# Half of the tokens of an expert layer computed densely over streamed tables, instead of gathering 128 expert rows for each token

## The reference

```
q = (hf @ w_q).reshape(T, 8, 2, 128)
s = jnp.einsum('thpd,hpnd->thpn', q, sub_keys)
sc, idx = lax.top_k(s, 16)
cand = sc[:, :, 0, :, None] + sc[:, :, 1, None, :]           # 256 sums a head
cidx = idx[:, :, 0, :, None] * 128 + idx[:, :, 1, None, :]
top_sc, pos = lax.top_k(cand, 16)
eidx = jnp.take_along_axis(cidx, pos, axis=-1)
gate = jax.nn.softmax(top_sc, axis=-1)
act = jax.nn.gelu(jnp.einsum('thkd,td->thk', u_tab[eidx], hf))
y = jnp.einsum('thk,thkd->td', gate * act, v_tab[eidx])
out = rms_norm(h + g2 * y, final_g)
```

## Time and profile before

| | |
|---|---|
| time, median of 3 runs | 3458.14 us (3454.32 to 3459.94) |
| span of the profiled execution | 3452.1 us |
| busy: PE, DVE, ACT, POOL | 91%, 60%, 31%, 56% of the span |
| last stage (first to last indirect DMA) | 2132.4 to 3416.6 us |
| DMA in the last stage | 411 GB/s |

### The profile page before, as it was taken

The page is one execution under the profiler, slowest core; times in us unless marked ns, Lnnn a source line. Parts: engine busy times, 40 slices in busy tenths (PEclk is TensorE's granted clock), DMA queues, the critical chain, the costliest instruction groups (busy, mean ns, idle before and its releaser), DMA issues.

```text
span 3452.1 us, 34902 instructions
## 1 busy us (share of the span) xinstructions
PE 3142.6 (91%) x12254; PEld 2099.6 (61%) x12254; DVE 2087.5 (60%) x3701; ACT 1062.6 (31%) x2577; POOL 1917.9 (56%) x1198
## 2 busy tenths in 40 slices
PE   7999999999999999999999999999978787777776
PEld 5778778887766888868777677544433333333332
DVE  5764453336764433479556776777667676666654
ACT  4564441112165211120132432333333332333222
POOL 4545259997403899968767565444444444434432
PEclk9999999999999999999999999999999999999999
DMA  4430022232311222323413124999999999999997
GB/s 164 171 134 1 13 86 98 97 120 74 134 62 49 90 95 96 115 71 124 140 62 115 50 80 172 421 421 419 422 415 412 421 421 421 421 421 420 421 421 299
DMA packets 108994, 741.68 MB, mean 215 GB/s; under 512 B 11816, under 2 KB 12968, under 8 KB 20776
## 3 DMA queue, kind: packets, MB, share of 16 engines
q0 software_dynamic: 73728, 536.90, 37.5%
q1 hardware_dynamic: 31488, 196.25, 16.2%
q10 hardware_dynamic: 3624, 6.56, 0.5%
HBM read 731.28 MB, written 8.39 MB: 214 GB/s over the span
## 4 chain that ended last, share of the span: by engine, by line
PE 63%; DMA 21%; DVE 8%; ACT 4%; issue 2%; POOL 2%; DVEq 0%; POOLq 0%; ACTq 0%
DMA arena<-in_peer_uv,rstd 15%; PE bank L1298 13%; PE bank L1299 13%; PE bank L1300 13%; PE bank L1814 8%; DMA weight_ring<-in_peer_uv,rstd 3%; DMA normed<-in_peer_uv,rstd 2%; DVE arena L3295 2%; PE bank L1829 1%; PE bank L1744 1%; PE bank L1726 1%; PE bank L1612 1%; PE bank L1490 1%; PE bank L1245 1%; PE bank L1500 1%
## 5 line engine op out<-in xcount | busy, mean ns | idle before, releaser
L1155 POOL DMA_INDIRECT arena<-in_peer_uv,rstd x419 | 456.4, 1089 | 622.0 <-PE bank L1814 570.3
L3295 DVE CUSTOM_DVE_ANT_0 arena<-arena,branch 128x1024 f32<-128x1024 f32 x419 | 510.5, 1225 | 333.5 <-DMA arena<-in_peer_uv,rstd 327.5
L1300 PE MATMUL bank<-split_arena 128*128 128x512 f32 x1776 | 695.1, 391 | 0.0
L1066 POOL TENSOR_TENSOR split_arena<-weight_ring,ones 128x1024 fp32r<-128x1024 f32 x204 | 506.6, 2483 | 151.0 <-PE bank L1300 99.3
L1298 PE MATMUL bank<-split_arena 128*128 128x512 f32 x1392 | 546.6, 393 | 5.6 <-DVE split_normed L2697 2.5
L1299 PE MATMUL bank<-split_arena 128*128 128x512 f32 x1392 | 542.3, 390 | 0.0
L1068 POOL TENSOR_TENSOR split_arena<-weight_ring,split_arena 128x1024 fp32r<-128x1024 f32 x204 | 519.3, 2545 | 16.0
L1814 PE MATMUL bank<-arena,row_diagonals 128*128 128x512 f32 x836 | 397.8, 618 | 92.0 <-ACT row_diagonals L2425 91.7
L1814 PE MATMUL bank<-arena,level_mask 128*128 128x512 f32 x840 | 392.0, 608 | 75.0 <-ACT level_mask L2425 74.7
L1300 PEld LDWEIGHTS bank<-split_arena 128*128 128x128 f32 x1776 | 334.0, 188 | 73.6
L1035 POOL TENSOR_TENSOR split_arena<-weight_ring,split_arena 128x1024 fp32r<-128x1024 f32 x54 | 129.5, 2406 | 401.2 <-ACT split_arena L1980 349.3
(11 more groups left out here) (490 smaller groups left out, 4921.4 us busy)
## 6 DMA issues: line engine op xcount, KB each, us to landing
weight_ring<-in_w_up SPq DMA_DIRECT2D x32, 1024.0 KB, 4.9
weight_ring<-in_w_down SPq DMA_DIRECT2D x32, 1024.0 KB, 4.9
weight_ring<-in_w_in SPq DMA_DIRECT2D x32, 1024.0 KB, 5.0
weight_ring<-in_ada_w SPq DMA_DIRECT2D x24, 1024.0 KB, 4.9
weight_ring<-in_w_in_a SPq DMA_DIRECT2D x12, 1024.0 KB, 6.4
weight_ring<-in_w_out SPq DMA_DIRECT2D x12, 1024.0 KB, 6.9
weight_ring<-in_w_in_b SPq DMA_DIRECT2D x10, 1024.0 KB, 5.9
arena<-in_peer_uv,rstd POOLq DMA_INDIRECT x419
```

The costliest lines, as they stand in the source:

```text
L1066: pool.tensor_tensor(hi, part, bc_mid(ones[:], DT), ALU.mult).then_inc(split_hi, 1)
L1155: pool.indirect_dma_start(row_slots[slot_of[r]], None, a["peer_uv"], bass.IndirectOffsetOnAxis(ap=experts[n % 2][:, c:c + 1], axis=0)).the ...
L1300: return pe.matmul(psum[t.bank][:], hi, a_lo[k], start=False, stop=last)
L3295: dve.tensor_tensor_reduce(row, row, h_tok[:, r // NE, :], 1.0, 0.0, ALU.mult, ALU.add, dots[:, i % 4, j:j + 1]).then_inc(dot_ready, 1)
```

## The change

Blocks 0 and 1 (256 tokens) still gather their 256 rows. Blocks 2 and 3 (256 tokens, `DENSE`) are computed against all 16384 experts: u and v are laid out a second time, as 128 units each of 128x1024 (512 KB; unit j holds the experts whose second key is j), and stream through four buffers (`raws`). ScalarE copies a unit to its high part (`raw_top`), GpSimd subtracts for the low part (`raw_rest`, since `low_by` returns 0 for every unit), and TensorE multiplies: `up_unit` has 24 fp32r matmuls of 256 columns, `down_unit` 12 of 512. Between the two stand Gelu (`activate`) and the product with a dense matrix of gates, zero where a token has not chosen an expert. That matrix is made by 64 "gate" steps: one-hot matrices of the first key by GpSimd (`first_ones`, 8 instructions) and of the second by VectorE (`second_ones`), scaled by ScalarE, multiplied on TensorE, and folded in by VectorE (`gate_weights`).

The program of the last stage is now: 32 groups of two rows as before (64 rows, all of block 0, with all query work for all blocks packed beside them), and then 320 steps in the list `STEPS`: 64 u units (steps 0 to 63); 32 gate steps (64 to 95); 64 v units and 64 u units in turn (96 to 223); 32 gate steps (224 to 255); 64 v units (256 to 319). The other 192 rows ride along in them, by `row_step`: 24 in steps 4 to 63, 12 in the first gate steps, 96 in steps 96 to 223, 12 in the second gate steps, and 48 in the 56 steps from 256. These late rows have 2, then 3, then 4 slots, and their second half is now VectorE's (`late_add`) instead of TensorE's. Of the searches, 59 pieces stand beside the 32 groups, and 66 pieces at one a step from step 0.

```diff
-NROW = TT * NE
-NGRP = NROW // GROUP
+SUMMED = 64
+NGRP = SUMMED // GROUP
+LATE = 2 * NE - SUMMED
+DENSE = 2 * P
+RAWS = 4
+PAIRS = 3
...
+        piece_count = [1 if 2 <= i <= 12 else 0 if i in (0, 13, 14) else 2 if i <= 21 else 3 if i <= 27 else 4 for i in range(NGRP)]
...
+                    low_wait(sp, n - RAWS)
+                sp.dma_start(raws[n % RAWS], a["peer_vd" if value else "peer_ut"][m]).then_inc(raw_landed[n % RAWS], 16)
...
+            def raw_rest(n):
...
+                hi, lo = pairs_of[n % PAIRS]
+                pool.wait_ge(raw_high, n + 1)
+                pool.tensor_tensor(lo, raws[n % RAWS], f32(hi), ALU.subtract).then_inc(raw_low[0], 1)
...
+            def late_gather(x):
...
+                if before is not None:
+                    pool.wait_ge(late_acc, before + 1)
...
+                pool.indirect_dma_start(late_slots[i], None, a["peer_uv"],
...
+                for x in range(GTOK):
+                    m = pool.tensor_scalar(one_first[v % 2][:, x, :], iota_key, index_t[b][:, 0, GTOK * t + x:GTOK * t + x + 1], None,
+                                           ALU.is_equal)
...
+            for s, (kind, v) in enumerate(STEPS):
+                if kind == "item":
+                    raw_rest(v + 2)
+                else:
+                    first_ones(v)
+                for x in gathers_at[s]:
+                    late_gather(x)
...
+                for k in range(DT):
...
+                    pe.matmul(psum[t.bank][:, 0:DENSE], hi[:, k, :], dense_hi[:, k, :], start=k == 0, stop=False)
+                    pe.matmul(psum[t.bank][:, 0:DENSE], hi[:, k, :], dense_lo[:, k, :], start=False, stop=False)
+                    m = pe.matmul(psum[t.bank][:, 0:DENSE], lo[:, k, :], dense_hi[:, k, :], start=False, stop=k == DT - 1)
...
+                for b in range(2):
+                    for w, part in ((w_hi, hi), (w_hi, lo), (w_lo, hi)):
+                        for c in range(2):
+                            x = pe.matmul(psum[2 * b + c][:], blk(w, b), part[:, 512 * c:512 * (c + 1)],
...
+                act.wait_ge(raw_landed[n % RAWS], 16 * (n // RAWS + 1))
+                if n >= PAIRS:
+                    act.wait_ge(item_done, n - PAIRS + 1)
...
+                act.activation(pairs_of[n % PAIRS][0], raws[n % RAWS], ACT.Copy).then_inc(raw_high, 1)
...
+                dve.tensor_tensor(w_lo, weights[:, :, m % WHALF], f32(w_hi), ALU.subtract).then_inc(w_low, 1)
...
+                dve.wait_ge(late_landed[gather_slot[x]], 16 * gather_fill[x])
+                dve.tensor_tensor_reduce(row, row, h_tok[:, n, :], 1.0, 0.0, ALU.mult, ALU.add,
+                                         late_dots[:, x % 8:x % 8 + 1]).then_inc(late_dot, 1)
...
+                dve.wait_ge(late_gate, x + 1)
...
+                    m = dve.scalar_tensor_tensor(acc[n], row, w, acc[n], ALU.mult, ALU.add)
```

More of the change, by code:

```diff
@@ L105, in build @@
         ring = sb("weight_ring", [P, RING, UNIT_K * UNIT_N])
+        with nc.sbuf_tensor("split_residual", [P, DT, SEQ], F32R) as split_X:
+            pass
         X = sb("residual", [P, DT, SEQ])
@@ L562, in build @@
                 n, x = turn_at[i]
[L563 to L573 removed]
+                tok_turns[n].append(aux(2 + x))
@@ new lines, in build, with item_of @@
+            for n, g in score_at.get(i, ()):
+                plan_scores(n, g, 4 + g % 2)
+        LAST_SCORES = [(2, 3, 6), (3, 3, 7), (1, 0, 2), (1, 1, 3)]
+        for n, g, bank in LAST_SCORES:
+            plan_scores(n, g, bank)
+        def item_of(m, value):
+            if not value:
+                return m if m < WHALF else m + (m - WHALF) + 1
+            return WHALF + 2 * m if m < WHALF else NKEY + m
+        ITEMS = [None] * (2 * NKEY)
+        for m in range(NKEY):
+            ITEMS[item_of(m, False)] = (False, m)
+            ITEMS[item_of(m, True)] = (True, m)
@@ new lines, in build @@
+        G_FIRST = {0: item_of(0, True), 1: item_of(WHALF, True)}
+        STEPS = []
+        for n in range(2 * NKEY):
+            for half, at in G_FIRST.items():
+                if n == at:
+                    STEPS += [("gate", half * NGATE + q) for q in range(NGATE)]
+            STEPS.append(("item", n))
+        step_of = {x: s for s, x in enumerate(STEPS)}
+        V_LAST = step_of["item", G_FIRST[1]]
+        late_score_at = {10: (1, 2, 6), 18: (1, 3, 7)}
+        index_at = {21: 0, 35: 1}
@@ L576, in build @@
+        v_tiles = [item_tile(2 * NKEY - 1, b) for b in range(4)]
         q_f = region(0, LH)
@@ new lines, in build @@
+        G_AT = [step_of["gate", half * NGATE] for half in range(2)]
+        row_step = []
+        for first, last, count_ in ((4, G_AT[0], 24), (G_AT[0], G_AT[0] + NGATE, 12), (G_AT[0] + NGATE, G_AT[1], 96),
+                                    (G_AT[1], V_LAST, 12), (V_LAST, V_LAST + 56, 48)):
+            row_step += [first + i * (last - first) // count_ for i in range(count_)]
+        first_gather = {0: -1, 1: -1, 2: 22, 3: G_AT[0]}
+        gather_step = [first_gather[gather_slot[x]] if gather_prev[x] is None else row_step[gather_prev[x]] + 2 for x in range(LATE)]
@@ new lines, in gate_products @@
+            def gate_products(v):
+                t = gate_tiles[v]
+                pe.wait_ge(first_hot, v + 1)
+                pe.wait_ge(gate_hot, v + 1)
+                free(pe, t)
+                for x in range(GTOK):
+                    m = pe.matmul(psum[t.bank][:, x * WHALF:(x + 1) * WHALF], one_first[v % 2][:, x, :], one_second[v % 2][:, x, :],
+                                  start=True, stop=True)
+                m.then_inc(psum_full, 1)
+            for s, (kind, v) in enumerate(STEPS):
+                if kind == "gate":
+                    gate_products(v)
+                elif ITEMS[v][0]:
+                    down_unit(v, ITEMS[v][1])
+                else:
+                    up_unit(v, ITEMS[v][1])
+                if s in late_score_at:
+                    key_scores(*late_score_at[s][0:2])
+                if s in index_at:
+                    b = index_at[s]
+                    pe.wait_ge(turn_in, sum(k[0] >= 2 and searched[k] <= searched[2 + b, 3] for k in SEARCHES))
+                    turn(index_tiles[b], [firsts[2 + b], seconds[2 + b], gates[2 + b]])
+                if s == GAIN_AT:
@@ L3312, in _ @@
-            add_rows(TT - 1)
-            finish_rows(TT - 1)
+                pieces(i)
+            for k in range(DT):
+                dve.wait_ge(dense_high, k + 1)
+                dve.tensor_tensor(dense_lo[:, k, :], H[:, k, DENSE:], f32(dense_hi[:, k, :]), ALU.subtract).then_inc(dense_split, 1)
+            for x, t in enumerate(row_sums):
+                full(dve, t)
+                dve.tensor_copy(acc[0][:, 512 * x:512 * (x + 1)], psum[t.bank][:]).then_inc(bank_out[t.bank], 1)
+            for t in row_sums:
+                have(dve, t)
```

632 lines of the change are left out of this document (455 added, 177 removed).

## The result

The changed kernel takes 3966.51 us (median of 4 runs, 3964.59 to 3970.1) against 3458.71 us for the kernel before, measured beside it: a ratio of 1.1472 [1.1456, 1.1488], 14.7% slower. The forecast was 3790 us, with a range to 3900. The direction was right; the time is 176 us over the forecast and 67 us over the range.

A forecast was written before the change was run, and what follows sets the result against it. DMA bound the last stage before; then VectorE and GpSimd taking turns would. 2141.6 + 240 + 12 + 275 + 211 + 584 + 302 + 18 = 3784 us, with 6 us around it 3790 us; range 3660 to 3900.

The forecast's parts named there:

- the 3.25 us: Average time for each of the 320 steps at which the whole time would stay as it was.
- The 32 groups and the bubble: Start of the last stage: 240 us for 32 two-row groups, then 12 us until the first units reach TensorE.
- Turns of VectorE and GpSimd: In the 320 steps, two-input VectorE instructions and GpSimd subtractions exclude each other; a 512-element instruction costs the pair 0.54 us.
- Steps 96 to 223: 128 units, 96 rows and 64 weight splits: 4.56 us a step, 584 us (545 to 666).
- the gate steps: 64 steps making the dense gates: chain of 3.3 us a step, one-hot instructions 2.4 for eight; 211 us (166 to 256).
- The rival on the clock: TensorE falls to 1.2 GHz from idling: units of 5.2 to 5.6 us, 4030 us in all; chance 0.03.
- Steps 256 to 319: Last 64 units, 48 rows in the first 56: 5.0 us a step, then 8 x 2.8; 302 us (284 to 341).
- late adds... low parts behind those, then TensorE: In the steps, later VectorE adds would delay gathers in GpSimd's queue, then low parts, then TensorE; no size given.
- Steps 0 to 63: First 64 units with 24 rows and 64 pieces of searches: 4.3 us a step, 275 us (240 to 326).
- The expectation on halves: With every second low part on VectorE: 3.9, 3.8 and 4.6 us a step, 3810 us in all.
- theory C: In steps 96 to 223, which VectorE instruction waits behind a subtraction counts: 3.8 to 3.9 us a step, 3840 us in all.
- The rival of tighter turns: Over all 320 steps, each subtraction precedes a waiting VectorE instruction and gathers wait under products: 3870 to 4010 us; chance 0.17.

The follow-up runs named there:

- e3: Changed kernel with all low parts but the first two subtracted by VectorE, not GpSimd: 3816.13 us, 1.1034 of the kernel before.
- e2: Changed kernel with products and adds of the 192 late rows replaced by one-input sums (part of the result left out): 3803.93 us, one run.
- e1: Changed kernel with first-key one-hot matrices made by one VectorE instruction a gate step, not eight of GpSimd: 3870.39 us, 1.1195 of the kernel before.
- e10: e1 with half of the gate matmuls (gates of half of the dense tokens left out): 3814.47 us, 1.1033 of the kernel before.
- e5: Changed kernel with a late row's ScalarE work one step later and its add behind the next product: 3950.61 us, 1.1428 of the kernel before.
- e4: Changed kernel with every second low part, after the first two, subtracted by VectorE: 3925.85 us, 1.1354 of the kernel before.
- e7: Changed kernel with low parts of v units alone subtracted by VectorE, u units by GpSimd: 3890.05 us, 1.1253 of the kernel before.
- e8: Changed kernel with the edits of e1, e5 and e7 together: 3705.73 us, 1.0718 of the kernel before.

## Why the prediction was wrong

- **Direction and bound.** Right. DMA ceased to be the bound, and a step costs more than the 3.25 us that would have kept the time.
- **The 32 groups and the bubble.** TensorE began the first unit at 2378.0 us instead of 2393.6, 16 us better than forecast. It was idle for 6.0 us before it, where 12 were put. What it waited for in this bubble is a VectorE instruction of 32 elements, held as long as GpSimd subtracted (VectorE, then GpSimd):

```profile
2370.29 7.26 DVE L3574 TENSOR_TENSOR rstd<-squares 128x32 f32<-128x32 f32 x1
...
2370.54 4.66 POOL L1289 TENSOR_TENSOR split_residual<-weight_ring,split_residual 128x1024 fp32r<-128x1024 f32 x2
2375.14 2.34 POOL L1289 TENSOR_TENSOR split_arena<-weight_ring,split_arena 128x1024 fp32r<-128x1024 f32 x1
```

  Its median over the run is 0.19 us. It began 0.25 us before the first of three subtractions, got no turn between them, and ended 0.07 us after the third. In e3, with two subtractions there, it took 4.97.
- **Turns of VectorE and GpSimd.** Right, and shown: e2 takes the second input away, and e3 the subtractions, and either gives back 150 to 163 us. Steps 96 to 223 took 4.39 against 4.56 us. TensorE was 74% busy there at a clock of 0.94, not near 60% at full clock, but it was not the bound. For the semaphores (0.4 in the gate steps, and in the 0.9 behind a product) the forecast had no row; the trace has VectorE idle for 0.60 us behind a product. The forecast spread the waits over the product, the add and a small part of the splits; in the trace the splits and adds have them, and VectorE also waits before the splits.
- **The step that failed: the gate steps.** "The one-hot instructions of GpSimd have no row; 128 elements at the rate of L1035 are 0.30 us, 2.4 for eight, and 0 to 2.4 bound it." They take 0.593, 4.74 for eight. The rate per element of a 1024-element instruction was carried down to 128 elements, and from a subtraction of two tensors to a TENSOR_SCALAR. The instruction takes 0.29 us more than that. Whether this is a fixed cost of each instruction or a slower rate of this one, no run tells, as all have the same size. And the estimate was made the upper bound as well, so that the range had no room for it, though the forecast itself counted the gate steps among its weakest terms. GpSimd's sum, 4.74 + 0.4 for gathers, went over the chain of 3.3, and the bound moved to another engine. e1, which takes it away, gives back 84 us; e2, which takes the turns away, 41.
- **The clock in the gate steps**, the second part of the same term. "TensorE 16 x 0.117 = 1.9" took full clock; the granted clock is 0.50 in both stretches and the 16 records of a step take 3.6. The rival on the clock was weighed for the unit steps, where it came in small part (0.87 to 0.94), and not for the gate steps. It was no bound while GpSimd took 4.74. Without that a step takes 4.6, and e10 shows that TensorE has a share in it; with 3.6 us of TensorE for each step at this clock, 3.3 was out of reach in any case.
- **Steps 256 to 319.** 37 us too low. The sum added up turns, while a loop through four queues takes 5.64 us for each step with a row; e5 breaks it for 32 us. The forecast had the way in which a wait spreads ("late adds... low parts behind those, then TensorE") but gave it no price.
- **Steps 0 to 63.** 17 us too low; VectorE busy 276 of 292 us. Against e3, the durations of its instructions other than subtractions add up to 90 us more: 30 in the products and adds of rows, and 60 in instructions of the searches, of which TENSOR_SCALAR and CAST read one tensor. The forecast had put 0.5 us a step for a piece's two-input instructions.
- **The expectation on halves** (e4, and theory C of e7) failed too: that of e4 took waits as proportional to the number of subtractions. The account of VectorE's queue above fits e3, e4 and e7 within 3 us, but it is read from their own traces. In e8 it gives 150 us for 63 subtractions, 2.4 each.
- **The rival of tighter turns.** The measured time lies in its range (3870 to 4010), but not by its mechanism: it had 326, 256, 666 and 341 us for the four parts, and 292, 379, 561 and 339 were measured.

A gather beside VectorE was weighed in the prediction. In e7 one begins under a product that ends at 3104.61, another under a plain TENSOR_TENSOR that ends at 3114.65 (VectorE, then GpSimd):

```profile
3101.19 3.42 DVE L3669 CUSTOM_DVE_ANT_0 weight_ring<-weight_ring,branch 128x1024 f32<-128x1024 f32 x1
3112.38 2.27 DVE L3625 TENSOR_TENSOR split_residual<-weight_ring,split_residual 128x1024 fp32r<-128x1024 f32 x1 [1.03 <-ACT split_residual L2719]
...
3100.98 2.54 POOL L1289 TENSOR_TENSOR split_residual<-weight_ring,split_residual 128x1024 fp32r<-128x1024 f32 x1 [0.79 <-ACT split_residual L2719]
3103.68 1.76 POOL L1304 DMA_INDIRECT arena<-in_peer_uv,rstd  x1 [0.16 <-issue]
3113.71 1.76 POOL L1304 DMA_INDIRECT weight_ring<-in_peer_uv,rstd  x1 [0.16 <-issue]
```

Both take 1.76 us and end 0.82 to 0.83 us after VectorE's instruction. A gather takes 1.28 us in steps 96 to 223 of the changed kernel and 1.71 in e3, where GpSimd has no subtractions to do, against 1.005 in e2, where rows have one input. The Trainium skill (SBUF — State Buffer, Who interferes with whom) infers that a two-input instruction doesn't hold up the generation of descriptors. The traces show that it holds up the indirect DMA. That instruction also reads its row numbers (`rstd`) from SBUF, and no run tells whether it is this read or the generation that was held. The section's rule that a two-input instruction contends with GpSimd's reads agrees with e2 and e3.

## What to carry to other kernels

- Before moving work to the engine that looks idle, count what it costs the other engine in waiting. A GpSimd subtraction of 2.4 us cost VectorE 1.8 to 2.2 us where both read SBUF; doing it on VectorE cost 1.14, though the two engines were about equally busy (449 and 476 of 561 us).
- Don't scale a duration down in proportion to the elements, or over to another operation: 0.30 us was worked out so for the one-hot instruction, and it took 0.593. Eight of them cost GpSimd 4.74 us, and one of 1024 on VectorE 1.22. A price without a row needs an upper bound well above its estimate, above all where the engine would then pass the present chain.
- When two engines take turns, an order that removes a gap gains only if nobody used the gap: 0 us with the subtractions on GpSimd, some 65 without.
